# Three of four squared MLP blocks turned by VectorE and SBUF transfers instead of TensorE

## The chip, the core and the metric

The kernel runs on 1 core of one Trainium2 chip. The metric is device time in microseconds (us): median 2288.86 of 3 runs (2288.14 to 2289.62). Engines are named as the profile does: PE is TensorE (PEld its weight loads), DVE VectorE, ACT ScalarE, POOL GpSimd, SP SyncE; SPq, POOLq and ACTq are the queues from which an engine issues DMAs.

## The reference, cut to what matters

Two transformer blocks on one sequence of 256 tokens, width 2048, float32. The change lies in the MLP of the first:

```python
u = _rmsnorm(h, norm_mlp_g)                     # (256, 2048)
a = jnp.einsum('bsd,df->bsf', u, w_up)          # (256, 8192)
a = jnp.square(jax.nn.relu(a))
h = h + jnp.einsum('bsf,fd->bsd', a, w_down)    # back to (256, 2048)
```

Before it come the first block's projection, Fourier mixing and attention; behind it the second block: gated linear attention, a convolution and a SwiGLU, with six modulation vectors made from `c @ w_mod` (2048 x 12288).

## The kernel before, in words

**Products.** Every large product is made of groups: a group is 512 rows of a weight matrix by 512 columns, 1 MB, which SP loads in two pieces of 512 KB (`load`, L380) into a ring of 4 groups (`wring`). ACT rounds a piece to `whi` (L575 or L565), DVE makes the remainder `wlo` (L1090), and PE does, for each piece, 4 matmuls of 128x512 with hi times `whi` (L1798), 4 with lo times `whi` (L1802) and 4 with hi times `wlo` (L1807). `whi` and `wlo` hold two groups. So SP may load a group when DVE is done with the one four before (`lo_done`, L382), and ACT may round a piece when PE has finished the same piece two groups before (`piece_multiplied`, L574).

**The MLP.** It runs in `MLP_CHUNKS` = 4 chunks of 32 groups (`mlp_chunk`, on ACT L839, DVE L1383, PE L2056). In this text "group 0" to "group 31" are those of a chunk in the order in which PE multiplies them. Groups 0 to 15 are four blocks of `w_up` (`j` = 0 to 3, four groups each, operand `ahi`/`alo`). After each of them ACT writes relu of the sums to `blk2` (L823) and the square of that to `blk` (L827), 256 tokens by 512 columns. Groups 16 to 31 are four blocks of `w_down`; their operand `xhi`/`xlo` is the squared block with tokens in the free dimension, so the block must be turned. PE turns it: `turn_rows(blk, 2)` (L2081, eight 128x128 transposes at L1869) behind group 4j+1, for j = 1 to 4, that is behind groups 5, 9, 13 and 17. ACT rounds the two PSUM banks to `xhi` (L591), DVE takes the remainder `xlo` (L1152). Group 16 multiplies block 0, group 17 block 1, group 18 block 2, group 19 block 3, and so on for each column block.

**How far ahead ACT and DVE are.** The opening of the kernel (L697 to L709) has ACT and DVE do two groups more than PE, and they stay two ahead in their program order. Where the code of `mlp_chunk` says `g` on ACT and DVE, the group handled is group g+2. The turned block of j = 4 is therefore rounded (`g % 4 == 1`) behind ACT's rounding of group 19, whose second piece waits for PE to finish group 17.

**The modulation vectors.** Beside the MLP, POOL loads `w_mod` in steps of 512 KB into a ring of two (L460), and DVE adds each step to `macc` with `scalar_tensor_tensor` (L1116, L1120; 2 or 4 instructions a step). `MLP_MODS` gives the step behind each group on DVE, `MLP_REDUCED = {7: SC2, 15: SC1, 22: GT1, 30: SH2}` the groups behind which PE turns the finished `macc` (`reduce_mod`, L1873, L1880; it waits for `mod_acc`). SC1 has the double steps (4 instructions): they stand on DVE behind groups 9 to 16, and PE reduces them behind group 15.

**The second block's SwiGLU** already turns three of four blocks another way: DVE turns 32x32 squares (L1693), POOL moves the strips with sixteen transfers of 32 KB within SBUF (L551), ACT rounds the placed rows (L1018) and DVE takes the remainder (L1698).

Of the kernel before, what the change touches and what calls it, by code (L numbers as in the profile page):

```python
# [55 lines left out]
X_HI = 2 * (2 * KG - 1) + 4 * KG + 8 * MLP_CHUNKS + 2 * KG + 2 * KG + 8  # L56
# [54 lines left out]
def two_blocks(nc, x, ctx_in, w_in, w_fourier, w_out, w_up, w_down, w_mod, w_in2, w_out2, w_gate,  # L111
               w_up2, w_down2, vectors, gates_w, mid_g, final_g, tables, fourier_tables, attn_tables, out):
    ctx = ExitStack()
    with ctx:
# [91 lines left out]
        with ExitStack() as ph:  # L206
# [47 lines left out]
            sem(n) for n in ("squares_turned", "rows_moved", "moved_hi", "moved_lo"))  # L254
        out_s = sem("out_s")
# [112 lines left out]
        T_O = 8 + 8 + 8 * MLP_CHUNKS + 8 + 8 + 4 + BANKS["out"] + sum(  # L368
# [3 lines left out]
        MOVES = 16 * 16  # L372
        block = ctx.enter_context(nc.Block())
# [3 lines left out]
        def _(sp):  # L377
# [28 lines left out]
            with c.loop(sp, MLP_CHUNKS, g=32) as i:  # L406
                for j in range(4):
                    block_of(w_up, i * D + j * NB)
                for n in range(4):
                    block_of(w_down, n * NB, kg0=i * 4)  # L410
# [144 lines left out]
        def _(act):  # L555
# [262 lines left out]
            def relu_square(j, first=False):  # L818

                if first:  # L820
                    act.wait_ge(rstd_done, 2)
                for t in range(T):
                    last = act.activation(blk2[:, t, :], acc[:, 2 * (j % 2) + t, :], ACT.Relu, scale=rstd[:, 1, t:t + 1])  # L823
                last.then_inc(blk_half, 1)
                c.add("half")
                act.wait_ge(blk_half, c.at("half"))
                act.activation(blk[:, :, :], blk2[:, :, :], ACT.Square).then_inc(blk_ready, 1)  # L827
                c.add("blk")

# [9 lines left out]
            def mlp_chunk(first=False, last=False):  # L839

                def round_group(g):
                    round_piece(0)
                    if g - 1 in MLP_REDUCED and not (last and MLP_REDUCED[g - 1] == SH2):
                        sum_mod(MLP_REDUCED[g - 1] == SC1)
                    round_piece(1)
                    if last and g in CTX_TURNS:
                        round_modulated(ahi, CTX_TURNS[g], CTX_TURNS[g] + 1)

                for j in range(8):
                    round_group(4 * j)  # L850
                    if j >= 5:
                        square_block(j - 5, first)
                    round_group(4 * j + 1)
                    if first and j == 0:
                        root(1)
                    if 1 <= j <= 4:
                        round_banks(xhi, 4 * (j - 1), 2)
                    round_group(4 * j + 2)
                    round_group(4 * j + 3)
                    if j < 4:  # L860
                        wait_block(2)
                        relu_square(j, first and j == 0)
                square_block(3, first)
# [3 lines left out]
            with c.loop(act, MLP_CHUNKS - 1, 1, g=32, q=8, half=4, blk=4, ha=4, ssq=4 * T, mt=5):  # L867
                mlp_chunk()
# [211 lines left out]
        def _(dve):  # L1080
# [301 lines left out]

            def mlp_chunk(i, first=False, last=False):  # L1383
                done = 0
                for g in range(32):
# [7 lines left out]
                    if g % 4 == 1 and 1 <= j <= 4:  # L1393
                        remain_banks(xhi, xlo, 4 * (j - 1), 2)
# [25 lines left out]
            with c.loop(dve, MLP_CHUNKS - 1, 1, g=32, q=8, hi=8, m=32, ma=80, mt=5, msum=5 * KG) as i:  # L1420
# [346 lines left out]
        def _(pe):  # L1767
# [288 lines left out]
            def mlp_chunk(first=False, last=False):  # L2056
# [6 lines left out]
                for j in range(8):  # L2063
# [10 lines left out]
                    for kg in range(3):  # L2074
                        multiply(hi, lo, (kg,), 4, pair)
# [3 lines left out]
                        if kg == 1 and 1 <= j <= 4:  # L2079
# [13 lines left out]
                c.add("blk", 4)  # L2093

            mlp_chunk(True)
            with c.loop(pe, MLP_CHUNKS - 1, 1, g=32, q=8, ma=80, ha=4, half=4, blk=4):
# [331 lines left out]
```

## Time and profile before

| | |
|---|---|
| median of 3 runs | 2288.86 us |
| span of the profiled execution | 2285.8 us |
| what a run has around that span (difference of the two) | 3.1 us |
| PE busy | 2266.4 us (99%) |
| DVE busy, ACT busy | 1556.3 (68%), 1109.7 (49%) |
| granted PE clock, mean of the span | 0.997 |
| PE idle in the MLP | 1.0 us |

The page and the answers show one execution of the program. Its own device time stands nowhere apart from the span; the 3.1 us lie around the span. The MLP lasts from about 295 to about 1015 us. A row of a timeline gives the start, how long the merged instructions lasted from the first start to the last end, and how many they are; PE's matmuls overlap, so the distance between the starts of two rows is what a row costs. `[x <-E line]` behind a row is the engine's idle time before it and who ended it.

### The profile page before, as it was taken

The page shows a single profiled execution, that of the slowest core. Times are in us where ns is not written, and L with a number is a line of the kernel's source. Part 1 is how long each engine was busy: PE and PEld are TensorE (multiplying, and loading weights), DVE is VectorE, ACT ScalarE, POOL GpSimd, SP SyncE. Part 2 cuts the span into 40 slices and gives each one's busy share as a digit, 9 for nine tenths or more (in the row PEclk, how much of TensorE's full clock was granted, in tenths as well). Part 3 has the DMA queues.
Part 4 walks back from the last instruction along what each step waited for, and adds up shares of the span by engine and source line. Part 5 has one row for each costly group of instructions (what it writes and reads, how often), then busy time and mean ns, then how long its engine had stood idle before and what let it go on. Part 6 is the DMA issues. An engine that isn't in the chain of part 4 may idle for free.

```text
span 2285.8 us, 28964 instructions
## 1 busy us (share of the span) xinstructions
PE 2266.4 (99%) x10345; PEld 1864.5 (82%) x10345; DVE 1556.3 (68%) x1869; ACT 1109.7 (49%) x1531; POOL 223.5 (10%) x361
## 2 busy tenths in 40 slices
PE   9999999999999999999999999999999999999998
PEld 7888888888888888888878877787888888888886
DVE  7886778778867877887767664556555545555556
ACT  6446455555545545545463463545444344444444
POOL 0121001111111111110011000000210011100110
PEclk9999999999999999999999999999999999999999
DMA  8983679978888888886677664564665666656663
GB/s 311 331 272 97 206 235 320 317 267 293 275 281 287 273 301 269 272 280 215 220 242 245 209 203 129 186 220 158 210 203 194 207 207 198 207 185 201 195 195 126
DMA packets 250005, 528.12 MB, mean 231 GB/s; under 512 B 22144, under 2 KB 22544, under 8 KB 248592
## 3 DMA queue, kind: packets, MB, share of 16 engines
q1 hardware_dynamic: 214256, 405.32, 54.2%
q0 software_dynamic: 33664, 116.17, 14.8%
q10 hardware_dynamic: 1952, 4.85, 0.6%
q8 instruction: 84, 1.38, 0.2%
q14 instruction: 49, 0.40, 0.1%
HBM read 517.87 MB, written 4.21 MB: 228 GB/s over the span
## 4 chain that ended last, share of the span: by engine, by line
PE 97%; DVE 1%; ACT 1%; DMA 0%; issue 0%; SPq 0%; ACTq 0%; DVEq 0%; POOLq 0%
PE acc L1798 30%; PE acc L1807 29%; PE acc L1802 29%; PE tp L1869 2%; PE m L1880 1%; PE acc L1820 0%; PE acc L1825 0%; PE acc L1830 0%; PE tp L2206 0%; PE tp L2224 0%; PE tp L2218 0%; PE acc L2000 0%; PE tp L2131 0%; PE acc L1853 0%; PE acc L1851 0%
## 5 line engine op out<-in xcount | busy, mean ns | idle before, releaser
L1090 DVE TENSOR_TENSOR wlo<-wring,whi 128x1024 fp32r<-128x1024 f32 x762 | 919.5, 1216 | 562.6 <-ACT whi L565 455.4
L565 ACT ACTIVATE whi<-wring 128x1024 fp32r<-128x1024 f32 (+1 forms) x510 | 532.1, 1047 | 720.4 <-PE acc L1807 719.3
L1798 PE MATMUL acc<-whi,xhi 128*128 128x512 f32 x2056 | 558.5, 393 | 0.1
L1802 PE MATMUL acc<-whi,xlo 128*128 128x512 f32 x2056 | 550.0, 389 | 0.0
L1807 PE MATMUL acc<-wlo,xhi 128*128 128x512 f32 x2056 | 549.9, 389 | 0.0
L1802 PEld LDWEIGHTS acc<-whi,xlo 128*128 128x128 f32 x2056 | 386.0, 188 | 81.1
L1807 PEld LDWEIGHTS acc<-wlo,xhi 128*128 128x128 f32 x2056 | 386.0, 188 | 80.7
L1798 PEld LDWEIGHTS acc<-whi,xhi 128*128 128x128 f32 x2056 | 381.2, 188 | 86.3 <-issue 9.0
L575 ACT ACTIVATE whi<-wring 128x1024 fp32r<-128x1024 f32 x266 | 280.8, 1059 | 319.8 <-PE acc L1807 318.1
L1120 DVE SCALAR_TENSOR_TENSOR macc<-mring,csil,macc 128x512 f32<-128x512 f32 x480 | 344.0, 747 | 29.3 <-DMA mring<-w_mod 23.0
L460 POOL DMA_DIRECT2D mring<-w_mod x192 | 138.9, 724 | 1047.4 <-DVE macc L1120 998.9
L1798 PE MATMUL acc<-whi,ahi 128*128 128x512 f32 x608 | 164.9, 393 | 0.0
L1807 PE MATMUL acc<-wlo,ahi 128*128 128x512 f32 x608 | 162.8, 389 | 0.0
L1802 PE MATMUL acc<-whi,alo 128*128 128x512 f32 x608 | 162.7, 389 | 0.0
L1802 PEld LDWEIGHTS acc<-whi,alo 128*128 128x128 f32 x608 | 114.1, 188 | 24.1
L1807 PEld LDWEIGHTS acc<-wlo,ahi 128*128 128x128 f32 x608 | 114.1, 188 | 24.0
L1798 PEld LDWEIGHTS acc<-whi,ahi 128*128 128x128 f32 x608 | 112.3, 188 | 22.1 <-issue 0.2
L551 POOL DMA_DIRECT2D tmpT<-blk x128 | 62.6, 498 | 517.9 <-DVE blk L1693 516.6
L1798 PE MATMUL acc<-whi,bhi 128*128 128x512 f32 x336 | 90.1, 390 | 0.0
L1807 PE MATMUL acc<-wlo,bhi 128*128 128x512 f32 x336 | 89.8, 389 | 0.0
L1802 PE MATMUL acc<-whi,blo 128*128 128x512 f32 x336 | 89.8, 389 | 0.0
L1802 PEld LDWEIGHTS acc<-whi,blo 128*128 128x128 f32 x336 | 63.1, 188 | 13.1
(277 smaller groups left out, 1313.7 us busy)
## 6 DMA issues: line engine op xcount, KB each, us to landing
wring<-w_up SPq DMA_DIRECT2D x216, 512.0 KB, 4.7
wring<-w_down SPq DMA_DIRECT2D x216, 512.0 KB, 5.1
mring<-w_mod POOLq DMA_DIRECT2D x192, 512.0 KB, 5.3
wring<-w_in SPq DMA_DIRECT2D x184, 512.0 KB, 5.2
wring<-w_gate SPq DMA_DIRECT2D x88, 512.0 KB, 4.3
wring<-w_out SPq DMA_DIRECT2D x64, 512.0 KB, 4.9
tmpT<-blk POOLq DMA_DIRECT2D x128, 32.0 KB, 3.4
gbig<-ctx_in POOLq DMA_DIRECT2D x2, 1024.0 KB, 8.1
```

The lines of the kernel that those rows point to most:

```text
L460: pool.dma_start(mring[:, c.slot("m", MSLOTS), :, :], w_mod_v[s, :, :, bass.ds(i * NB + kind * D, NB)])\
L551: pool.dma_start(placed[32 * j:32 * j + 32, i, :], strips[32 * i:32 * i + 32, j, :]).then_inc(rows_moved, 16)
L565: act.activation(whi[:, piece_slot(c, piece), 0:half], wring[:, g4, piece * half:(piece + 1) * half], ACT.Copy).then_inc(hi_done, 1)
L575: act.activation(whi[:, piece_slot(c, piece), :], wring[:, g4, piece * half:(piece + 1) * half], ACT.Copy).then_inc(hi_done, 1)
L1090: dve.tensor_tensor(wlo[:, h4, 0:half], wring[:, g4, piece * half:(piece + 1) * half], whi[:, h4, 0:half].bitcast(F32), ALU.subtract).then ...
L1120: dve.scalar_tensor_tensor(macc[:, who, :], mring[:, m2, kt, :], csil[:, who, k:k + 1], macc[:, who, :], ALU.mult, ALU.add).then_inc(mod_a ...
L1798: pe.matmul(acc[:, 2 * pair + t, :], hi[:, tile, t * P:(t + 1) * P], whi[:, h4, w], start=(tile == starts), stop=False)
L1802: pe.matmul(acc[:, 2 * pair + t, :], lo[:, tile, t * P:(t + 1) * P], whi[:, h4, w], start=False, stop=False)
L1807: last = pe.matmul(acc[:, 2 * pair + t, :], hi[:, tile, t * P:(t + 1) * P], wlo[:, h4, w], start=False, stop=(tile == stops))
L1869: last = pe.transpose(tp[:, q, j * S + t * P:j * S + (t + 1) * P], src[:, t, f:f + P], ident)
L1880: last = pe.transpose(bank[:, j * P:(j + 1) * P], macc[:, who, j * P:(j + 1) * P], ident)
```

## The change: blocks 0 to 2 are turned on DVE and moved by SP

Block 3 of each chunk stays on PE (behind group 17). Blocks 0, 1 and 2 go another way. ACT writes relu and square both in `blk`. DVE turns the block in 32x32 squares into `blk2` (`turn_relu`, two instructions), behind its remainders of groups 7, 11 and 15. SP, behind its loads of groups 9, 13 and 17, waits for that and issues sixteen transfers of 32 partitions by 1 KB from `blk2` to `tmpT` (`move_strips`). ACT rounds the placed rows in four instructions (`round_relu`) behind groups 11, 15 and 19, and DVE takes four remainders (`remain_relu`) behind the same groups. PE waits for `relu_lo` before group 16 (blocks 0 and 1) and before group 18 (block 2).

```diff
@@ sync
+            def move_strips():
+                sp.wait_ge(relu_turned, c.at("rs", T, T))
                 for j in range(4):
-                    block_of(w_up, i * D + j * NB)
+                    for i in range(4):
+                        sp.dma_start(placed[32 * j:32 * j + 32, i, :], strips[32 * i:32 * i + 32, j, :]).then_inc(relu_moved, 16)
+                c.add("rs")
+            def up_block(i, j):
+                v = w_up.rearrange("(g k p) n -> g p k n", k=KG, p=P)
+                for kg in range(KT // KG):
+                    load(v[kg, :, :, bass.ds(i * D + j * NB, NB)])
+                    if j >= 2 and kg == 1:
+                        move_strips()
...
                 for n in range(4):
-                    block_of(w_down, n * NB, kg0=i * 4)
+                    v = w_down.rearrange("(g k p) n -> g p k n", k=KG, p=P)
+                    for kg in range(KG):
+                        load(v[bass.ds(i * 4 + kg, 1), :, :, n * NB:(n + 1) * NB].rearrange("a p k n -> (a p) k n"))
+                        if n == 0 and kg == 1:
+                            move_strips()
@@ scalar
+                if j:
+                    act.wait_ge(relu_turned, c.at("rt", T, T))
+                    c.add("rt")
                 for t in range(T):
-                    last = act.activation(blk2[:, t, :], acc[:, 2 * (j % 2) + t, :], ACT.Relu, scale=rstd[:, 1, t:t + 1])
+                    last = act.activation(blk[:, t, :], acc[:, 2 * (j % 2) + t, :], ACT.Relu, scale=rstd[:, 1, t:t + 1])
...
+            def round_relu(tile):
+                act.wait_ge(relu_moved, c.at("rm", RELU_MOVES, RELU_MOVES))
+                for k in range(KG):
+                    act.activation(xhi[:, tile + k, :].rearrange("p (t i b) -> p t i b", t=T, i=4),
+                                   moved[:, k], ACT.Copy).then_inc(relu_hi, 1)
+                c.add("rm")
...
-                    if 1 <= j <= 4:
-                        round_banks(xhi, 4 * (j - 1), 2)
+                    if 2 <= j <= 4:
+                        round_relu(4 * (j - 2))
+                    if j == 4:
+                        round_banks(xhi, 12, 2)
@@ vector
+            def turn_relu():
+                dve.wait_ge(blk_ready, c.at("blk", 1))
+                dve.wait_ge(relu_moved, c.at("rt", 0, RELU_MOVES))
+                for t in range(T):
+                    dve.transpose(turned[:, t], blk[:, t, :].rearrange("p (k j b) -> p k j b", k=KG, j=4)).then_inc(relu_turned, 1)
+                c.add("rt")
+            def remain_relu(tile):
+                for k in range(KG):
+                    dve.wait_ge(relu_hi, c.at("rk", 1))
+                    dve.tensor_tensor(xlo[:, tile + k, :].rearrange("p (t i b) -> p t i b", t=T, i=4), moved[:, k],
+                                      xhi[:, tile + k, :].bitcast(F32).rearrange("p (t i b) -> p t i b", t=T, i=4),
+                                      ALU.subtract).then_inc(relu_lo, 1)
+                    c.add("rk")
...
                     if g % 4 == 1 and 1 <= j <= 4:
-                        remain_banks(xhi, xlo, 4 * (j - 1), 2)
+                        if j >= 2:
+                            remain_relu(4 * (j - 2))
+                        if j < 4:
+                            turn_relu()
+                        c.add("blk")
+                        if j == 4:
+                            remain_banks(xhi, xlo, 12, 2)
@@ tensor
+                        if j == 4 and kg in (0, 2):
+                            pe.wait_ge(relu_lo, c.at("rs", KG * (2 if kg == 0 else 3), KG))
                         multiply(hi, lo, (kg,), 4, pair)
...
-                        if kg == 1 and 1 <= j <= 4:
+                        if kg == 1 and j == 4:
                             pe.wait_ge(blk_ready, c.at("blk", j))
                             turn_rows(blk, 2)
```

The counts of the bank semaphores follow (`X_HI`, `T_O`, `q`, `hi`). Where instructions stand now is shown at two places. First DVE from its remainders of group 15 to the last SC1 step, behind those of group 16, first chunk, before (the `macc` rows are the last two of the eight steps that PE's reduction behind group 15 waits for):

```order
L1090 TENSOR_TENSOR wlo<-wring,whi 128x1024 [waits hi_done] x2
L1152 TENSOR_TENSOR xlo<-tp,xhi 128x512 [waits tp_hi] x2
L1120 SCALAR_TENSOR_TENSOR macc<-mring,csil,macc 128x512 [waits mod_acc,step_landed0]
L1120 SCALAR_TENSOR_TENSOR macc<-mring,csil,macc 128x512 [waits mod_acc] x3
L1090 TENSOR_TENSOR wlo<-wring,whi 128x1024 [waits hi_done] x2
L1120 SCALAR_TENSOR_TENSOR macc<-mring,csil,macc 128x512 [waits mod_acc,step_landed1]
L1120 SCALAR_TENSOR_TENSOR macc<-mring,csil,macc 128x512 [waits mod_acc] x3
```

And the same stretch now:

```order
L1126 TENSOR_TENSOR wlo<-wring,whi 128x1024 [waits hi_done] x2
L1430 TENSOR_TENSOR xlo<-tmpT,xhi 128x256 [waits relu_hi] x4
L1424 STREAM_TRANSPOSE blk<-blk 128x4x4x32 [waits relu_moved,blk_ready]
L1424 STREAM_TRANSPOSE blk<-blk 128x4x4x32
L1156 SCALAR_TENSOR_TENSOR macc<-mring,csil,macc 128x512 [waits mod_acc,step_landed0]
L1156 SCALAR_TENSOR_TENSOR macc<-mring,csil,macc 128x512 [waits mod_acc] x3
L1126 TENSOR_TENSOR wlo<-wring,whi 128x1024 [waits hi_done] x2
L1156 SCALAR_TENSOR_TENSOR macc<-mring,csil,macc 128x512 [waits mod_acc,step_landed1]
L1156 SCALAR_TENSOR_TENSOR macc<-mring,csil,macc 128x512 [waits mod_acc] x3
```

The one pair of bank remainders (L1152 before, now L1188) has become four remainders of the moved block 1 and two turns of block 2, ahead of the last two SC1 steps.

Second PE behind group 17, first chunk, before:

```order
L1869 MATMUL tp<-tabs,blk 128x128 [waits tp_free,blk_ready]
L1869 MATMUL tp<-tabs,blk 128x128 x3
L1869 MATMUL tp<-tabs,blk 128x128 [waits tp_free]
L1869 MATMUL tp<-tabs,blk 128x128 x3
L1798 MATMUL acc<-whi,xhi 128x512 [waits hi_done]
L1798 MATMUL acc<-whi,xhi 128x512 x3
L1802 MATMUL acc<-whi,xlo 128x512 x4
L1807 MATMUL acc<-wlo,xhi 128x512 [waits lo_done]
```

And the same place now:

```order
L1928 MATMUL tp<-tabs,blk 128x128 [waits tp_free,blk_ready]
L1928 MATMUL tp<-tabs,blk 128x128 x3
L1928 MATMUL tp<-tabs,blk 128x128 [waits tp_free]
L1928 MATMUL tp<-tabs,blk 128x128 x3
L1857 MATMUL acc<-whi,xhi 128x512 [waits hi_done,relu_lo]
L1857 MATMUL acc<-whi,xhi 128x512 x3
L1861 MATMUL acc<-whi,xlo 128x512 x4
L1866 MATMUL acc<-wlo,xhi 128x512 [waits lo_done]
```

The first matmul of group 18 has gained a wait, for `relu_lo`. What gives it stands on DVE here, behind the remainders of group 19:

```order
L1126 TENSOR_TENSOR wlo<-wring,whi 128x1024 [waits hi_done] x2
L1430 TENSOR_TENSOR xlo<-tmpT,xhi 128x256 [waits relu_hi] x4
L1188 TENSOR_TENSOR xlo<-tp,xhi 128x512 [waits tp_hi] x2
L1156 SCALAR_TENSOR_TENSOR macc<-mring,csil,macc 128x512 [waits mod_acc,step_landed0]
L1156 SCALAR_TENSOR_TENSOR macc<-mring,csil,macc 128x512 [waits mod_acc]
```

The four remainders of block 2 (L1430) follow the two remainders of group 19 (L1126), and those of block 3 (L1188) follow them.

## Rows read from the trace of the kernel before

**Rows 1.** The page: span, busy times, granted clock, the chain that ended last.

```profile
span 2285.8 us, 28964 instructions
...
PEclk9999999999999999999999999999999999999999
...
PE 97%; DVE 1%; ACT 1%; DMA 0%; issue 0%; SPq 0%; ACTq 0%; DVEq 0%; POOLq 0%
```

**Rows 2.** Waits in 290 to 1010 us: who waited, us in total, times, longest.

```profile
PE m L1880 <- DVE macc L1120: 1.0, 1, 1.0
```

**Rows 3.** Timeline of PE round group 17 of the second chunk: start us, us.

```profile
600.90 1.07 PE L1807 MATMUL acc<-wlo,xhi 128*128 128x512 f32 x4
601.81 1.03 PE L1869 MATMUL tp<-tabs,blk 128*128 128x128 f32 x8
602.60 1.17 PE L1798 MATMUL acc<-whi,xhi 128*128 128x512 f32 x4
603.61 1.07 PE L1802 MATMUL acc<-whi,xlo 128*128 128x512 f32 x4
```

**Rows 4.** Timeline of ACT and DVE in the same place.

```profile
602.01 1.06 ACT L575 ACTIVATE whi<-wring 128x1024 fp32r<-128x1024 f32 x1 [1.66 <-PE acc L1807]
603.10 1.23 DVE L1090 TENSOR_TENSOR wlo<-wring,whi 128x1024 fp32r<-128x1024 f32 x1 [0.99 <-ACT whi L575]
604.24 1.28 DVE L1152 TENSOR_TENSOR xlo<-tp,xhi 128x512 fp32r<-128x512 f32 x2
```

**Rows 5.** Timeline of DVE in the SwiGLU, where blocks are moved.

```profile
1634.78 1.42 DVE L1698 TENSOR_TENSOR blo<-tmpT,bhi 128x256 fp32r<-128x256 f32 x4
1646.90 1.30 DVE L1693 STREAM_TRANSPOSE blk<-blk 128x512 f32<-128x512 f32 x2
1648.13 1.18 DVE L1090 TENSOR_TENSOR wlo<-wring,whi 128x1024 fp32r<-128x1024 f32 x1
```

**Rows 6.** Timeline of DVE, groups 11 to 16 of the second chunk, and PE's reduction.

```profile
556.83 1.23 DVE L1090 TENSOR_TENSOR wlo<-wring,whi 128x1024 fp32r<-128x1024 f32 x1 [0.36 <-ACT whi L575]
559.17 2.73 DVE L1120 SCALAR_TENSOR_TENSOR macc<-mring,csil,macc 128x512 f32<-128x512 f32 x4
575.19 2.73 DVE L1120 SCALAR_TENSOR_TENSOR macc<-mring,csil,macc 128x512 f32<-128x512 f32 x4
577.84 1.22 DVE L1090 TENSOR_TENSOR wlo<-wring,whi 128x1024 fp32r<-128x1024 f32 x1
587.00 2.73 DVE L1120 SCALAR_TENSOR_TENSOR macc<-mring,csil,macc 128x512 f32<-128x512 f32 x4
590.01 1.04 PE L1880 MATMUL m<-tabs,macc 128*128 128x128 f32 x8
```

**Rows 7.** DMA issues: SP's (ns min/median/max), POOL's sixteen (timeline), landing of SP's loads.

```profile
L387 SPq DMA_DIRECT2D wring<-w_up x216: 367/373/1625, 292.7 to 2181.1; - x108
1692.02 7.81 POOL L551 DMA_DIRECT2D tmpT<-blk  x16 [35.71 <-DVE blk L1693]
wring<-w_down SPq DMA_DIRECT2D x8, 512.0 KB, 6.1
```

**Rows 8.** Timeline of PE: a pause in the attention, and the SwiGLU's opening.

```profile
196.47 0.63 PE L2025 MATMUL tp<-tabs,blk 128*128 128x128 f32 x4 [1.33 <-ACT blk L782]
1547.50 0.66 PE L2305 MATMUL m<-tabs,u_ffn 128*128 128x128 f32 x4 [1.07 <-DVE h L1618]
1549.64 0.98 PE L2305 MATMUL tp<-tabs,u_ffn 128*128 128x128 f32 x4 [1.49 <-DVE u_ffn L1645]
1552.05 2.07 PE L1820 MATMUL acc<-whi,xhi 128*128 128x512 f32 x4 [0.57 <-ACT xhi L600]
1557.03 1.07 PE L1820 MATMUL acc<-whi,xhi 128*128 128x512 f32 x4
```

**Rows 9.** Stretches of that opening: us, PE PEld DVE ACT POOL busy, PEclk, DMA share, GB/s.

```profile
1550.00:1552.00 2.00, 1.47 (x7) 1.07 (x6) 1.67 (x4) 0.88 (x2) 0.00 (x0) 0.50 0.00 0
1556.00:1558.00 2.00, 2.00 (x9) 1.61 (x8) 1.64 (x2) 0.33 (x1) 0.00 (x0) 0.84 0.86 277
```

More of the change, by code:

```diff
@@ L55 @@
 WARM = 4
-X_HI = 2 * (2 * KG - 1) + 4 * KG + 8 * MLP_CHUNKS + 2 * KG + 2 * KG + 8
+MLP_MOVED = 3
+X_HI = 2 * (2 * KG - 1) + 4 * KG + 2 * MLP_CHUNKS + 2 * KG + 2 * KG + 8
 H0 = 2
@@ L254, in two_blocks @@
             sem(n) for n in ("squares_turned", "rows_moved", "moved_hi", "moved_lo"))
+        relu_turned, relu_moved, relu_hi, relu_lo = (
+            sem(n) for n in ("relu_turned", "relu_moved", "relu_hi", "relu_lo"))
         out_s = sem("out_s")
@@ L366, in two_blocks @@
         BANKS = {"z": 1, "suffix": 1, "ctx_state": 1, "state": 2, "turn": 1, "out": 1, "conv": 2}
-        T_O = 8 + 8 + 8 * MLP_CHUNKS + 8 + 8 + 4 + BANKS["out"] + sum(
+        T_O = 8 + 8 + 2 * MLP_CHUNKS + 8 + 8 + 4 + BANKS["out"] + sum(
             BANKS.get(step[0], 0) for steps in BESIDE[1].values() for step in steps)
@@ L372, in two_blocks @@
         MOVES = 16 * 16
+        RELU_MOVES = 16 * 16
         block = ctx.enter_context(nc.Block())
@@ L405, in _ @@
                     block_of(w_out, i * (2 * NB) + j * NB)
-            with c.loop(sp, MLP_CHUNKS, g=32) as i:
+            def move_strips():
+                sp.wait_ge(relu_turned, c.at("rs", T, T))
                 for j in range(4):
-                    block_of(w_up, i * D + j * NB)
-                for n in range(4):
-                    block_of(w_down, n * NB, kg0=i * 4)
+                    for i in range(4):
[7 more added lines that the diff above has]
+                        move_strips()
+            with c.loop(sp, MLP_CHUNKS, g=32, rs=MLP_MOVED) as i:
+                for j in range(4):
+                    up_block(i, j)
+                for n in range(4):
+                    v = w_down.rearrange("(g k p) n -> g p k n", k=KG, p=P)
[3 more added lines that the diff above has]
+                            move_strips()
             for names in (C_IN, X_IN):
@@ L826, in relu_square @@
                 act.wait_ge(blk_half, c.at("half"))
-                act.activation(blk[:, :, :], blk2[:, :, :], ACT.Square).then_inc(blk_ready, 1)
+                act.activation(blk[:, :, :], blk[:, :, :], ACT.Square).then_inc(blk_ready, 1)
                 c.add("blk")
+            def round_relu(tile):
[4 more added lines that the diff above has]
+                c.add("rm")
             def square_block(n, first):
@@ L866, in _ @@
             root_and_scale(2, u_g, u_g)
-            with c.loop(act, MLP_CHUNKS - 1, 1, g=32, q=8, half=4, blk=4, ha=4, ssq=4 * T, mt=5):
+            with c.loop(act, MLP_CHUNKS - 1, 1, g=32, q=2, half=4, blk=4, ha=4, ssq=4 * T, mt=5, rt=MLP_MOVED, rm=MLP_MOVED):
                 mlp_chunk()
@@ L1419, in _ @@
             norm_scale(2, u_g, u_g)
-            with c.loop(dve, MLP_CHUNKS - 1, 1, g=32, q=8, hi=8, m=32, ma=80, mt=5, msum=5 * KG) as i:
+            with c.loop(dve, MLP_CHUNKS - 1, 1, g=32, q=2, hi=2, m=32, ma=80, mt=5, msum=5 * KG, blk=4, rt=MLP_MOVED,
+                        rk=KG * MLP_MOVED) as i:
                 mlp_chunk(i)
@@ L2093, in mlp_chunk @@
                 c.add("blk", 4)
+                c.add("rs", MLP_MOVED)
             mlp_chunk(True)
-            with c.loop(pe, MLP_CHUNKS - 1, 1, g=32, q=8, ma=80, ha=4, half=4, blk=4):
+            with c.loop(pe, MLP_CHUNKS - 1, 1, g=32, q=2, ma=80, ha=4, half=4, blk=4, rs=MLP_MOVED):
                 mlp_chunk()
```

## The prediction

> **What bounds the kernel now.** I read the page first: the chain that ended last is 97% PE and the granted clock is full in every slice [rows 1]. So PE's own instructions set the time, and one that is taken from PE is worth its full length as long as PE finds its operands. I then read the waits inside the MLP: PE waits once in 720 us, 1.0 us, for DVE's `macc` [rows 2]. The reader is to see two things: PE has no slack to give, and the only engine it ever waits for there is DVE with the modulation steps. So I asked of each edit what it takes from PE, and then at each wait of PE how near DVE and ACT already are, by laying the timelines of PE, ACT and DVE side by side in the second chunk.
>
> **What is removed.** Behind group 17 the turn is eight transposes. PE starts them at 601.81, the next matmuls at 602.60 and the ones after those at 603.61; a plain row of four takes 0.91 (600.90 to 601.81) [rows 3]. From 601.81 to 603.61 are 1.80; less 0.91, a turn costs 0.89. Three of four turns go in each of four chunks: 12 x 0.89 = 10.7 us off PE.
>
> **What DVE gets.** In place of two bank remainders it has, behind group 7 the two square turns, behind 11 and 15 four remainders and two turns, behind 19 four remainders more than before. The SwiGLU has the same instructions: four remainders 1.42, two turns 1.23 (1646.90 to 1648.13) [rows 5]; the bank remainders took 1.28 by their row [rows 4], less the 0.08 by which instructions overlap on DVE (a row of 2.73 is followed 2.65 later [rows 6]), 1.20. Behind groups 11 and 15 that is 1.42 + 1.23 - 1.20 = 1.45 more each, behind 7 nothing.
>
> **First place: PE's reduction behind group 15.** PE starts it at 590.01, and the last SC1 step on DVE runs from 587.00 to 589.73 [rows 6]: a margin of 0.28 now. With the change PE arrives earlier by three turns, 2.69, at 587.32. DVE arrives so: its second remainder of group 11 starts 0.90 earlier than 556.83 (one turn, behind group 5, is gone from PE, which ACT and DVE follow), at 555.93. From there DVE finds all inputs ready and is never idle. A remainder costs 1.14 (603.10 to 604.24) [rows 4], a double step 2.65 (575.19 to 577.84) [rows 6]. Group 11: 1.14 + 1.42 + 1.23 + 2.65 = 6.44. Groups 12, 13, 14: each 2 x 1.14 + 2.65 = 4.93, 14.79. Group 15: 2 x 1.14 + 1.42 + 1.23 + 2.65 = 7.58. Group 16: 2 x 1.14 + 2.73 = 5.01. Sum 33.82, end at 589.75. So the step ends where it ended before, and PE waits 589.80 - 587.32 = 2.5 us. The earlier turns bought nothing but a wait: 4 x 2.5 = 10.0 us. The idle time that DVE had between these groups (0.36 in the row of 556.83) is the only cover, and the sum has used it.
>
> **Second place: group 18.** PE's first matmul of group 18 waits for the remainders of block 2. ACT handles that block behind its rounding of group 19, whose second piece waits for PE's end of group 17 (ACT starts at 602.01, released by L1807) [rows 4]. DVE takes the remainder of that piece at 603.10 and would start on the block at 604.24; with four remainders of 1.42 it ends at 605.66, and PE goes on at about 605.71. PE, with the turn of block 3 done, would have gone on at 602.60 [rows 3]. That is 3.1 us of idling, which no amount of lead on SP or DVE can shorten, because it begins with PE's own end of group 17. The pattern is the same in all four chunks: 4 x 3.1 = 12.4 us. Block 3 follows on DVE at 605.7 and is wanted behind group 18: hidden.
>
> **SP's queue.** Each block costs SP a wait and sixteen issues. The wait itself holds the next load: load 14 may be issued when group 10's remainders are done, but stands behind the sixteen transfers, which wait for DVE's turn of block 1 at 559.7 (555.93 + 1.14 + 1.42 + 1.23 = 559.72). An issue takes 0.37 by SP's own rows, and 0.49 as POOL does sixteen in 7.81 [rows 7]: 5.9 to 7.8 us. SP comes free at 565.7 to 567.6, and the two pieces of load 14 land, at up to 6.1 [rows 7], by 571.5 to 574.2. DVE wants their rounded form at 572.25 and 573.39. So this costs DVE's dense run between 0 and 1.5 us, and PE's wait behind group 15 grows by as much. PE itself wants group 14 later than that. I take 0.7, near the middle, since the two issue rows lie equally near: 4 x 0.7 = 2.8. Loads 10 and 18 have the same delay but no dense run behind them; ACT's rounding of group 19 is reached in time. The transfers move 512 KB a block beside 1 MB a group; the transfers of the SwiGLU keep no PE waiting in the trace.
>
> **Back.** The one wait of 1.0 for `macc` [rows 2] comes late in the last chunk and goes, since PE arrives later there: -1.0.
>
> **The sum without the clock.** -10.7 + 10.0 + 12.4 + 2.8 - 1.0 = +13.5.
>
> **The clock.** PE idled 1.07 and 1.49 within 4 us at the SwiGLU's opening, with only transposes between, and the granted clock then stood at 0.50, the 1.2 GHz level, from 1550 until into the stretch from 1556 (0.84) [rows 8, 9]. At that level three rows of four 128x512 matmuls took 1552.05 to 1557.03, 4.98, where 3 x 0.91 = 2.73 is usual: 2.3 us lost. A pause of 1.33 in the attention brought no fall [rows 8 and 1]. The new pauses, 2.5 and 3.1, lie between: as long as the two of the opening together, but single. A fall can cost nothing, or 2.3 as here, or up to half of the 7 us at 0.5, 3.4. Of the eight pauses I let two be followed by a fall, because the longer kind is nearer to what the opening shows and its place differs from chunk to chunk: 2 x 2.3 = 4.6.
>
> By the Trainium skill, page "TensorE: Matmul & The Clock Gate", part "PE-mode transpose", transposes do not count as work for the clock gate as matmuls do. The turn of block 3 stands directly before the pause at group 18 and the reduction's transposes directly behind the one at group 15, so by that rule every pause is longer than its idle time and all eight could be followed by a fall; the opening, where only transposes broke the pause, agrees. That is the second rival.
>
> **Forecast.** +13.5 + 4.6 = +18.1 on the span of 2285.8, 2303.9, and with the 3.1 around it (the difference of span and median) 2307.
>
> **Rivals.**
> 1. Only the two waits, no fall and no late load: 13.5 - 2.8 = +10.7, 2299.6. For it: single pauses never brought a fall in this trace. Against it: none of them was as long.
> 2. All pauses are followed by a fall: 13.5 + 8 x 2.3 = +31.9, 2321. For it: the opening [rows 8, 9]. Against: the pause of 1.33.
> 3. DVE keeps up and only group 18 waits: -10.7 + 12.4 - 1.0 = +0.7, 2289.6, no change. It decides by whether DVE ends SC1 by 587.3; it would have to do 33.8 us of work in 31.4.
> 4. The other side: the remainders of block 2 are ready before PE ends group 17, because ACT's order is not two groups ahead as I read it, or PE's count is met by an earlier block. Then PE only waits behind group 15, -10.7 + 10.0 - 1.0 = -1.7, 2287.2, and with rival 3 in force as well -10.7, 2278. It decides at one point, whether ACT's rounding before the block is that of group 19. Rows 4 speak against it: ACT's rounding in front of the banks starts with PE's end of group 17.
> 5. SP's transfers are slower than POOL's, say twice, 15.6 us a block: loads 10, 14 and 18 come 8 later and PE itself waits about 4 at each: 12 x 4 = 48 more, some 2355. No row shows such an issue but the longest, 1.6 [rows 7].
>
> **Chances.** Forecast (two waits, one to four falls, loads a little late) 0.55; rival 1, 0.16; rival 2, 0.13; rival 3, 0.07; rival 4, 0.05; rival 5, 0.04. A measurement can tell about 0.2%, 4.6 us, from no change: below 2284.3 is faster, above 2293.4 slower. Faster has rival 4's larger half, 0.03; the same has the rest of it and rival 3's, 0.08; slower the rest, 0.89. For the range I take rival 1's end with a fall of the waits by a few us, 2296, and rival 2's end, 2322; outside are rivals 3, 4 and 5.
>
> **What would show it.** In the profile after: PE idle before L1939 (`m<-tabs,macc`) by DVE's `macc`, four times, 2.5 to 4 each; PE idle before L1857 in front of group 18 by DVE's `xlo` L1430, four times, 3.1; PE's transposes of `blk` in the MLP down from 128 to 32; SP's rows L415, 192 of them, near 0.4 each; the clock below 9 in slices of the MLP if falls come. No idle time before group 18 would refute the second place, and idle time there above 5 would mean late transfers or loads. If PE's idle time before L1939 is under 1, DVE had more room than its rows show. Idle time of PE released by `whi` or by a load would speak for rival 5.

## The result, and the profile after

The changed kernel takes 2355.68 us (median of 4 runs, 2354.0 to 2357.8) against 2289.24 for the kernel before on the same chip (4 runs): ratio 1.0289, 95% interval 1.0275 to 1.0303. It is slower by 66 us, where 18 were forecast, and outside the forecast range. The page after, against [rows 1] (the last row is the chain that ended last):

```profile
span 2353.7 us, 29072 instructions
...
PE 2282.5 (97%) x10249; PEld 1871.6 (80%) x10249; DVE 1571.5 (67%) x1917; ACT 1110.9 (47%) x1555; POOL 223.3 (9%) x361
...
PEclk9999999999899999989999999999999999999999
...
PE 81%; SPq 5%; DVE 5%; DMA 4%; issue 3%; ACT 2%; DVEq 0%; ACTq 0%; POOLq 0%
```

PE's share of the chain fell from 97% to 81%, and SP's queue, at 0% before, has 5%. The waits in 290 to 1080 us, against [rows 2] (who waited, us in total, times, longest):

```profile
ACT whi L598 <- DMA wring<-w_up: 74.6, 24, 11.6
ACT whi L598 <- DMA wring<-w_down: 42.1, 5, 11.6
PE m L1939 <- DVE macc L1156: 23.7, 5, 6.9
...
PE acc L1857 <- DVE xlo L1430: 15.4, 4, 4.2
PE acc L1857 <- ACT whi L598: 11.6, 5, 3.3
...
PE acc L1866 <- DVE wlo L1126: 1.6, 1, 1.6
```

PE waits 52.3 us in place of 1.0. The two waits forecast are there (23.7 and 15.4), and beside them 13.2 us for `whi` and `wlo`. The first two rows are the news: ACT now waits 116.7 us for loads of weights, which it never did in this stretch before.

PE in the second chunk, against [rows 3] and the last row of [rows 6]:

```profile
600.78 2.07 PE L1857 MATMUL acc<-whi,ahi 128*128 128x512 f32 x4 [2.87 <-ACT whi L598]
...
618.41 1.97 PE L1939 MATMUL m<-tabs,macc 128*128 128x128 f32 x8 [3.64 <-DVE macc L1156]
620.03 2.05 PE L1857 MATMUL acc<-whi,xhi 128*128 128x512 f32 x4
621.88 1.91 PE L1861 MATMUL acc<-whi,xlo 128*128 128x512 f32 x4
...
632.86 1.03 PE L1928 MATMUL tp<-tabs,blk 128*128 128x128 f32 x8
637.48 2.01 PE L1857 MATMUL acc<-whi,xhi 128*128 128x512 f32 x4 [3.58 <-DVE xlo L1430]
```

Three pauses in 40 us, and behind each a row of four matmuls takes 1.9 to 2.1 where [rows 3] have 1.07. The granted clock there (the stretch, its us, PE PEld DVE ACT POOL busy, PEclk, DMA share, GB/s, as in [rows 9]) is 0.50, the 1.2 GHz level:

```profile
618.00:622.00 4.00, 3.59 (x13) 3.21 (x14) 3.77 (x5) 0.11 (x1) 0.72 (x1) 0.50 0.50 133
```

SP's queue in that chunk, and its issue times (ns min/median/max) against [rows 7]:

```profile
557.68 10.52 SPq L415 DMA_DIRECT2D tmpT<-blk  x16
568.46 5.04 SPq L391 DMA_DIRECT2D wring<-w_up  x8
584.23 10.42 SPq L415 DMA_DIRECT2D tmpT<-blk  x16
594.90 2.15 SPq L391 DMA_DIRECT2D wring<-w_up  x4
597.31 2.71 SPq L391 DMA_DIRECT2D wring<-w_down  x4
610.84 10.01 SPq L415 DMA_DIRECT2D tmpT<-blk  x16
...
L415 SPq DMA_DIRECT2D tmpT<-blk x192: 507/590/987, 360.7 to 1010.2; - x192
```

Sixteen transfers take SP 10.0 to 10.5 us, 0.65 each, not 5.9 to 7.8. Behind each of the first two sixteens, SP issues eight pieces of weights within 5 us: they were overdue. What that does on ACT and DVE:

```profile
572.25 1.06 ACT L598 ACTIVATE whi<-wring 128x1024 fp32r<-128x1024 f32 x1 [4.09 <-DMA wring<-w_up]
...
599.67 1.06 ACT L598 ACTIVATE whi<-wring 128x1024 fp32r<-128x1024 f32 x1 [9.28 <-DMA wring<-w_up]
...
581.57 1.43 DVE L1430 TENSOR_TENSOR xlo<-tmpT,xhi 128x256 fp32r<-128x256 f32 x4
582.91 1.29 DVE L1424 STREAM_TRANSPOSE blk<-blk 128x512 f32<-128x512 f32 x2
```

The first row is group 10, the second group 14. The four remainders and the two turns take what the SwiGLU's rows gave [rows 5].

**The loop.** The chain that ended last, read in this stretch (start us, us, what; steps between are left out), shows why this repeats:

```profile
584.23 0.52 SPq L415
...
594.90 0.38 SPq L391
595.46 5.45 DMA wring<-w_up
601.02 1.07 ACT whi L598
...
609.60 1.23 DVE blk L1424 x2
610.84 0.51 SPq L415
```

From the first transfer of block 1 (584.23) to that of block 2 (610.84) are 26.6 us: sixteen transfers until SP issues load 14 (594.90, 10.7); its pieces land and ACT rounds the second from 601.02 (6.1); DVE's remainders, modulation steps and its turn of block 2, in program order, until SP is released (9.8). PE needs 21.8 for the four groups of that round (eight pieces of 2.72). So each round is 4.8 longer than PE's work, and PE's lead over the loads is used up after one. The round before it, from block 0 (557.68) to block 1, is 26.6 long as well.

### The profile page after: what moved, and what is told of

It is laid out like the page before. It is cut to its first block, busy times and chain, and to the rows that moved or that the text cites. A ratio compares the mean times of both kernels' runs of the same rounds, so it can differ in the third digit from the quotient of the medians.

```text
span 2353.7 us, 29072 instructions
## 1 busy us (share of the span) xinstructions
PE 2282.5 (97%) x10249; PEld 1871.6 (80%) x10249; DVE 1571.5 (67%) x1917; ACT 1110.9 (47%) x1555; POOL 223.3 (9%) x361
## 3 DMA queue, kind: packets, MB, share of 16 engines
q1 hardware_dynamic: 223472, 411.63, 52.3%
## 4 chain that ended last, share of the span: by engine, by line
PE 81%; SPq 5%; DVE 5%; DMA 4%; issue 3%; ACT 2%; DVEq 0%; ACTq 0%; POOLq 0%
PE acc L1857 24%; PE acc L1861 24%; PE acc L1866 24%; SPq L415 5%; DMA wring<-w_up 2%; DVE macc L1156 2%; DMA mring<-w_mod 1%; DVE wlo L1126 1%; PE tp L1928 1%; ACT whi L598 1%; DMA wring<-w_down 1%; ACT m L636 1%; DVE xlo L1430 1%; DVE blk L1424 1%; PE acc L1879 0%
## 5 line engine op out<-in xcount | busy, mean ns | idle before, releaser
L1126 DVE TENSOR_TENSOR wlo<-wring,whi 128x1024 fp32r<-128x1024 f32 x762 | 917.7, 1216 | 616.9 <-ACT whi L588 454.7
L1857 PE MATMUL acc<-whi,xhi 128*128 128x512 f32 x2056 | 565.8, 397 | 15.5 <-DVE xlo L1430 15.4
L1857 PEld LDWEIGHTS acc<-whi,xhi 128*128 128x128 f32 x2056 | 385.6, 190 | 103.9 <-DVE xlo L1430 16.4
L1857 PE MATMUL acc<-whi,ahi 128*128 128x512 f32 x608 | 166.4, 396 | 11.6 <-ACT whi L598 11.6
```

The costliest lines, as they stand in the source:

```text
L1126: dve.tensor_tensor(wlo[:, h4, 0:half], wring[:, g4, piece * half:(piece + 1) * half], whi[:, h4, 0:half].bitcast(F32), ALU.subtract).then ...
L1857: pe.matmul(acc[:, 2 * pair + t, :], hi[:, tile, t * P:(t + 1) * P], whi[:, h4, w], start=(tile == starts), stop=False)
```

## The experiments

For each kernel in it the table has the median, the span of its profiled execution less 2285.8, and an account of that difference: the turns removed (-10.7), PE's waits in 290 to 1080 us less the 1.0 of before, and the slower clock, (1 - mean granted clock) x span, less the 6.9 of before (clock 0.997). A clock has three digits, so each product is good to 1.2 and the difference of two to 2.3. The span is that of one execution: in `e5`, `e7` and `e11` it was the slowest of its kernel, so there it stands 4 to 6 us further from the kernel before than the median does.

| kernel | median | span, more | waits | clock (mean) | sum |
|---|---|---|---|---|---|
| after | 2355.7 | +67.9 | +51.3 | +30.8 (0.984) | +71.4 |
| e1_no_transfers | 2309.9 | +22.0 | +20.9 | +9.3 (0.993) | +19.5 |
| e2_transfers_later | 2311.6 | +25.1 | +22.7 | +11.6 (0.992) | +23.6 |
| e3_block2_sooner | 2337.9 | +47.1 | +40.2 | +16.4 (0.990) | +45.9 |
| e4_both | 2295.1 | +6.1 | +11.2 | +4.6 (0.995) | +5.1 |
| e5_reduction_later | 2299.2 | +17.8 | +16.7 | +11.5 (0.992) | +17.5 |
| e6_half_transfers | 2318.1 | +29.9 | +27.0 | +11.6 (0.992) | +27.9 |
| e7_one_transfer | 2314.3 | +30.6 | +25.4 | +13.9 (0.991) | +28.6 |
| e9_reductions_later | 2279.6 | -7.9 | +0.7 | +2.2 (0.996) | -7.8 |
| e11_no_transfers_reductions_later | 2278.0 | -4.8 | +1.8 | +2.3 (0.996) | -6.6 |

The account closes within 4 us for each, so nothing large is outside these three terms.

**No transfers.** SP neither waits nor issues, and ACT and DVE no longer wait for the strips to land (`relu_moved`); all their instructions stay, on rows that nothing has placed.

```diff
-                sp.wait_ge(relu_turned, c.at("rs", T, T))
-                for j in range(4):
-                    for i in range(4):
-                        sp.dma_start(placed[...], strips[...]).then_inc(relu_moved, 16)
...
-                act.wait_ge(relu_moved, c.at("rm", RELU_MOVES, RELU_MOVES))
...
-                dve.wait_ge(relu_moved, c.at("rt", 0, RELU_MOVES))
```

> The changed kernel without its 192 transfers of strips on SP and without the waits for them (SP neither waits nor issues; ACT and DVE still do all their instructions, on rows that nothing has placed). Theory (SP's queue: each block holds the next loads by SP's wait for the turn plus sixteen issues of 0.65 us, 10.4 in all, the weights come late, and DVE's steps before the reduction come late with them): the idle times before groups 10 to 14 go, the wait before the reduction behind group 15 falls from 3.6 to 6.9 to the 2.5 that DVE's own added work makes, the one before group 18 stays at 3.6 to 4.2; 2300 to 2312. Rival (DVE's added work, not SP, makes the wait before the reduction): it stays at 4 to 7 and the time stays above 2335.

2309.94 (ratio 1.0094, 1.0077 to 1.0110), in the range that was expected. Of the 66 us, some 45 go with the transfers. The landing of the strips, which this edit also took out of ACT's and DVE's way, is not what costs: in the changed kernel no wait of ACT or DVE in 290 to 1080 us ends with a `tmpT` transfer. What is left is what steps 1 to 3 of the prediction were about (steps are its parts: 1 what is removed, 2 the first place, 3 the second place, 4 SP's queue, 5 "Back"), and PE's rows in its second chunk show it. The wait before group 18 is shorter than the 3.6 to 4.2 expected here, 2.9 to 3.2:

```profile
597.42 1.09 PE L1933 MATMUL m<-tabs,macc 128*128 128x128 f32 x8 [2.10 <-DVE macc L1151]
...
613.18 1.90 PE L1851 MATMUL acc<-whi,xhi 128*128 128x512 f32 x4 [2.88 <-DVE xlo L1424]
```

**Transfers later.** The same sixteen transfers, behind loads 11, 15 and 19 in place of 9, 13 and 17 (`kg == 3` for `kg == 1` in both places).

> The sixteen transfers of a block stand two loads later on SP (behind the loads of groups 11, 15, 19 and not 9, 13, 17), so that SP no longer stands in a wait with two free places in the ring. Theory (the wait for the turn costs more than the issues): SP still loses 10.4 us to each block, but the loads behind it have some 8 us of room left, so PE never waits for whi or wring; the reduction waits about 2.5, group 18 waits for block 2: near the time of the run without transfers, within 8 us, 2300 to 2315, with a longer wait at group 18 if the transfers of block 2 end after PE's group 17. Rival (the issue time by itself makes loads late): 2335 to 2360.

2311.61 (1.0096, 1.0080 to 1.0113), in the range of the theory and 1.7 above the kernel without any, a difference inside the intervals. This kernel moves the same bytes over the same DMA engines as the changed one, so the traffic of the strips is not what costs 45 us either; their place in SP's queue is. SP in the second chunk:

```profile
547.52 11.22 SPq L415 DMA_DIRECT2D tmpT<-blk  x16
559.00 10.13 SPq L391 DMA_DIRECT2D wring<-w_up  x8
570.62 10.83 SPq L415 DMA_DIRECT2D tmpT<-blk  x16
581.72 9.64 SPq L391 DMA_DIRECT2D wring<-w_down  x8
```

Sixteen transfers take about as long as before (10.8 to 11.2), and eight loads behind them now take some 10 us to issue: they are no longer a burst but go out as their slots come free. Why two groups of place matter: block 1 is turned behind the remainders of group 11. Load 14, which stood behind its transfers, has its slot when group 10 is done, so it waited for a later event than its own and for 10.4 us of issue more. Load 16 has its slot when group 12 is done, and DVE ends that at 575.5, 5 us behind the turn (570.6): half of the issues fill time in which SP would have waited. The load then goes out 6 us behind its slot (581.7), and in this kernel ACT waits for no load of weights.

**One transfer, eight transfers.** At the changed kernel's place, `range(1)` and `range(1)`, or `range(4)` and `range(2)`, for the two loops over transfers, and `RELU_MOVES` to suit.

> The changed kernel with a single transfer per block, so that SyncE still waits for VectorE's turn at the same place, but issues for 0.65 us instead of 10.4 (the rest of each block stays unplaced). Theory (the 10.4 us of issue are what the loads have no slack for): 2306 to 2315, near the kernel without transfers (2309.9). Rival (the wait for the turn): over 2335.

> The changed kernel with 8 of a block's 16 transfers (half of each block stays unplaced), at the place that the change has. Theory (the loads are late by the wait for the turn and then the 10.4 us in which SyncE issues 16 transfers; without these 5.2 us most of it goes): load 14 lands about 5 us sooner, TensorE's waits for whi go and with them most of the slower clock, 2310 to 2328. Rival (waiting for the turn alone makes the loads late, the number of transfers doesn't matter): 2345 to 2356.

One transfer 2314.33 (1.0102, 1.0087 to 1.0118), eight 2318.13 (1.0128, 1.0112 to 1.0143), both where the theory had them. The kernel before was 1.4 slower in these two comparisons than in that of the kernel without transfers, so each is best taken over its own: 21.17 us without transfers, 24.15 with one, 27.95 with eight, 66.44 with sixteen. The wait for the turn with one issue costs 3.0, inside the intervals, the next seven 3.8 together, and the last eight 38.5. That is the loop: at eight, SP's part is 5.2 us in place of 10.7,

```profile
567.43 4.96 SPq L415 DMA_DIRECT2D tmpT<-blk  x8
572.64 2.11 SPq L391 DMA_DIRECT2D wring<-w_up  x4
```

so the chain of the round would be 26.6 - 5.5 = 21.1, an estimate just under PE's 21.8. The rounds as traced are 23.1 to 23.5, with eight transfers and with one: their length no longer hangs on the number of transfers. ACT's wait for weights is 12.4 us in place of 116.7.

**Block 2 sooner.** ACT rounds block 2 behind group 18, not 19, and DVE takes its remainders behind those of group 18.

```diff
-                    if 2 <= j <= 4:
+                    if 2 <= j <= 3:
                         round_relu(4 * (j - 2))
...
                     round_group(4 * j)
+                    if j == 4:
+                        round_relu(8)
...
+                    if g == 16:
+                        remain_relu(8)
```

> The changed kernel with ACT's rounding and DVE's remainders of block 2 one group sooner (behind group 18 in place of 19), nothing else. Theory: the 15.4 us of idle time before group 18 go, and the falls of the clock behind it with them (up to 2 to 3 us each): 2355 less 15 to 27, 2328 to 2342. Rival (PE would wait for late loads there anyway): 2350 to 2357.

2337.94 (1.0219, 1.0202 to 1.0236), as expected. PE's wait for the remainders of block 2 (`xlo`) goes from 15.4 to 2.0, the one for `macc` stays (26.5, from 23.7).

**Both of these.**

> Transfers two loads later and block 2 rounded one group sooner. What is left is the wait before the reduction behind group 15, about 2.5 a chunk, against 10.7 saved: if the clock does not fall 2287 to 2291, with a fall behind each of the four waits up to 2298. If block 2's transfers, now behind the load of group 19, end too late for the sooner place, PE waits some 2 to 4 before group 18 again: 2295 to 2310.

2295.07 (1.0028, 1.0017 to 1.0038), the end of the expectation with falls of the clock. One kind of wait is left, 12.2 us for `macc` in five places.

**Reduction later.** As both, with the reduction of SC1 behind group 16.

```diff
-                    **{g: (GT1, 2 if g == 18 else 1) for g in range(15, 22)},
+                    **{g: (GT1, 2 if g in (18, 20) else 1) for g in range(16, 22)},
-        MLP_REDUCED = {7: SC2, 15: SC1, 22: GT1, 30: SH2}
+        MLP_REDUCED = {7: SC2, 16: SC1, 22: GT1, 30: SH2}
```

> Transfers behind loads 11, 15 and 19, the third block rounded sooner, and the 32-step modulation group now runs behind groups 7 to 14 as before but is reduced behind group 16 (the next kind's steps follow from 16 on, two of them doubled). E4, the same without the last edit, took 2295.1 with 12.2 us of TensorE's wait for macc and about 4.6 us of slower clock more than before. Theory (VectorE is full only in the stretch up to group 16, one group more lets it catch up): both go, 2276 to 2284, faster than before. Rival (the wait is only pushed one group on, or to group 18): 2291 to 2298.

2299.16 (1.0042, 1.0029 to 1.0056): the theory missed, the rival came. PE's wait went, and came back behind group 22:

```profile
638.96 0.65 PE L1943 MATMUL m<-tabs,macc 128*128 128x128 f32 x4 [4.21 <-DVE macc L1158]
...
624.33 1.54 DVE L1158 SCALAR_TENSOR_TENSOR macc<-mring,csil,macc 128x512 f32<-128x512 f32 x2 [2.49 <-DMA mring<-w_mod]
```

With two doubled groups so near each other, DVE waits for the steps' own loads; `mring` has room for two.

**Reductions later.** The same with one doubled group for each kind:

```diff
+                    **{g: (GT1, 2 if g == 20 else 1) for g in range(16, 23)},
+                    **{g: (SH2, 2 if g == 27 else 1) for g in range(23, 30)}}
+        MLP_REDUCED = {7: SC2, 16: SC1, 23: GT1, 30: SH2}
```

> As E5 (transfers behind loads 11, 15 and 19, third block sooner, 32-step reduction behind group 16), but the next kind's steps run behind groups 16 to 22 with one of them doubled (at 20) and are reduced behind 23, and the last kind's behind 23 to 29 with one doubled (at 27). E5 took 2299.2: its wait for macc (16.3 us) had gone from the first reduction to the one behind group 22, ahead of which two steps in a row were doubled and VectorE waited for their loads. Theory (no group has then more steps than the loads follow): both waits go, with the slower clock behind them, 2276 to 2284, faster than before. Rival (the wait turns up at another group once more): 2290 to 2298.

2279.63 (5 runs, 2279.24 to 2281.20; ratio 0.9959, 0.9945 to 0.9972), 0.4% faster than the kernel before, as the theory had it. PE's waits in the stretch are 1.7 us in three places, and behind group 17 nothing is left between the turn of block 3 and group 18:

```profile
599.87 1.03 PE L1932 MATMUL tp<-tabs,blk 128*128 128x128 f32 x8
600.66 1.17 PE L1861 MATMUL acc<-whi,xhi 128*128 128x512 f32 x4
```

**What the transfers and the table are worth there.** The same without transfers, and the kernel before with only this table.

> E9 without its transfers (the third part of e1 and the moved reductions together; the turned squares are not put into place). Theory (at their new place the transfers cost next to nothing): within 3 us of E9, 2274 to 2283. Rival (48 transfers of 32 KB per chunk still delay the modulation loads or the weights): more than 5 us below E9.

> The kernel before (TensorE turns all four blocks), with only E9's table of modulation steps (reductions behind groups 16, 23 and 30). It tells whose the gain of E9 is (2279.6 against 2289.6). Theory (TensorE waits 1.0 us for macc in the kernel before, so the table has nothing to gain there, and E9's gain is that of the turns removed): 2287 to 2291. Rival (the table alone brings it): 2282 or less.

Without transfers 2278.04 (0.9948, 0.9933 to 0.9964): 1.6 less than with them, inside the intervals. The table alone 2290.83 (1.0005, 0.9996 to 1.0014): nothing. Both are as their theories had them. So the 10 us are those of the turns taken from PE. By the Trainium skill, page "VectorE: DVE Perf Modes", section "Rules for kernel authors", a 128x128 transpose goes to TensorE where PSUM will do as its target; here, where TensorE is the bound and DVE and SP have time, the other way is worth 10 us.

**Filled pauses.** TensorE multiplies the identity ahead of its waits, so that it does not pause.

```diff
+            def fill(n):
+                pe.wait_ge(tp_free, c.at("q", 1))
+                for _ in range(n):
+                    pe.matmul(tp[:, c.slot("q", 2), 0:P], ident, ident, start=True, stop=True)
```

> The changed kernel, with matmuls of the identity put in on TensorE ahead of the two waits: 28 (about 3.6 us) before the one for macc behind group 15, 26 (about 3.3 us) before the one for xlo at group 18, into the bank that the next turn uses. They add nothing to the result and stay within the waits as traced (3.6 to 6.9 and 3.6 to 4.2 us). Theory (the granted clock falls after TensorE has paused, and about 30 of the 67 us are matmuls at the lower clock): the falls behind these two waits go, 15 to 25 us come back, 2328 to 2342. Rival (the falls have another cause, or the waits for late loads bring them all the same): 2350 to 2362.

2382.13 (1.0403), outside both the theory and the rival, a miss of the experiment: each such matmul is two records, the fill of 28 took 6.4 us, and the one before group 18 waited itself for the bank of block 3's turn (20.4 us in four places). It shows only that the clock holds behind a filled pause. Again with 18, before the reduction alone:

> The changed kernel with fill ahead of the wait for macc behind group 15 only, 18 matmuls of the identity with itself, which ran as two records of 0.114 us each in E8, so about 4.1 us beside waits of 3.6 to 6.9 us. Nothing of it is in the result. E8 put in twice the length meant (6.4 us in one place, 5.9 behind another wait in the other). Theory (the clock falls after a pause; each of the four falls behind this wait costs 2.9 us, worked out from the rows at 618.41 us): 8 to 12 us come back, 2343 to 2348. Rival (the fall comes whether TensorE pauses there or not): 2354 to 2360.

2355.63 (1.0287, 1.0271 to 1.0302): nothing came back, though the clock did. The time is in the rival's range, but not for the rival's reason, that the fall comes all the same. The mean granted clock is 0.989 instead of 0.984, which by the account is 12 us. PE in its second chunk:

```profile
608.96 4.18 PE L2117 MATMUL tp<-tabs 128*128 128x128 f32 x36
615.51 1.09 PE L1940 MATMUL m<-tabs,macc 128*128 128x128 f32 x8 [2.37 <-DVE macc L1157]
...
634.85 2.07 PE L1858 MATMUL acc<-whi,xhi 128*128 128x512 f32 x4 [6.44 <-DVE xlo L1431]
```

The reduction's eight take 1.09, not 1.97; and the next wait, before group 18, is 6.4 instead of 3.6. Over the four chunks that wait grew from 15.4 to 24.6 us. The account closes here too: -10.7, waits +43.0, clock +19.0 and four fills of 4.1, together +67.7 against +67.4. So the chain through SP, ACT and DVE sets the pace between these two places, and PE at full clock only reaches the next wait sooner. That means that what the account puts down to the falls behind the reduction is not a saving to be had in the changed kernel. By the Trainium skill, page "TensorE: Matmul & The Clock Gate", section "HAM oscillation — how this bites in real kernels", PE restarts at the lower clock behind each wait for data and pays for it each time; the page says so of a kernel that waits for a DMA at each of its steps. The trace agrees in the three rows at 600.78, 618.41 and 637.48 us, but not behind every pause (2.08 us before 795.22 us is followed by a granted clock of 1.00); that PE pays each time, this run does not bear out where the next operand is late as well.

## Why the prediction was wrong

**Step 1, turns removed: right.** -10.7 was forecast. The best version has +0.7 of waits and +2.2 of clock in the account and is 7.9 shorter, which leaves 10.8 for the turns; the same without transfers leaves 8.9. Either is good to 2.3.

**Step 2, the wait before the reduction: mechanism and size right, by itself.** Forecast 2.5 in each chunk. Without transfers it is 2.09 to 2.15 in each. In the changed kernel it is 3.6 to 6.9, 22.0 in four, since ACT and DVE come to this stretch late. In the first chunk it is longer also where no load is late (3.83 with the transfers later, 4.71 with both edits); why was not tried.

**Step 3, the wait before group 18: right.** Forecast 3.1. Without transfers 2.88 to 3.21, 11.9 in four; in the changed kernel 15.4.

**Step 4, SP's queue: this failed.** The prediction gave it 2.8 us in all; the difference between the changed kernel and the one without transfers is 45.7 (45.3 with each taken over its own kernel before), of which the waits are 30.4. Without this term and with its clock term the prediction makes +15.3, where the kernel without transfers has +21.2; the rest of the miss is here. The step had two errors that matter. The price of an issue was taken from rows of other kinds, 0.37 (a load of 512 KB) and 0.49 (POOL); SP's small transfers take 0.65, so SP's part is 10.4 us. It also left out, in "DVE wants their rounded form", ACT's own rounding of a piece, 1.06 by [rows 4]. And it followed load 14 once, to DVE's dense run and no further ("loads 10 and 18 have the same delay but no dense run behind them"). But load 14 feeds the remainders and steps behind which DVE turns block 2, and that turn releases the next sixteen transfers and load 18. With the rest of the round as traced (26.6 - 10.7 = 15.9), even the forecast's issues of 5.9 to 7.8 would make 21.8 to 23.7 against PE's 21.8, an estimate: no slack, at the price assumed. Eight transfers against sixteen show how steep it is from there. Rival 5 named this end, "some 2355", with 0.04. Its time was met by chance: it wanted issues of 15.6 us a block and 4 us of PE's idling at each load; they took 10.4, and `whi` and `wlo` cost PE only 13.2.

**Step 5, the 1.0 back: wrong and small.** The late wait of the last chunk is there, 1.50 without transfers, 1.68 with.

**The clock.** Forecast 4.6, two falls in eight pauses. Without transfers the account has 9.3 (good to 2.3). There the four pauses of 2.9 to 3.2 before group 18 were each followed by rows of 1.80 to 2.07, and of the four of 2.1 before the reduction one was (411.04: the eight transposes at 1.09, the next row at 1.94): five falls of eight where the sum had two, so the term was too small by half even without late loads. The size of a fall, 2.3, was about right (9.3 / 5 = 1.9).

The length of a pause does not decide alone. In the four kernels without transfers, with them later, with one and with eight, all sixteen pauses of 2.87 to 3.21 before group 18 were followed by a fall, but only seven of the sixteen of 2.09 to 3.93 before the reduction. With eight transfers the reduction's pause of 3.84 is followed by rows of 1.17 and 1.08 (granted clock 1.00 from 411 to 414 us), the pause of 3.21 before group 18 by half clock (0.50 from 427 to 430).

Both kinds of pause stand beside eight transposes, before group 18 ahead of the pause and at the reduction behind it. So rival 2's rule, that transposes do not keep the clock up, is not settled: all pauses before group 18 go with it, more than half of those before the reduction do not.

The prediction's list of what would show it served: idle time of PE released by `whi`, named there as a sign for rival 5, is in the profile, and SP's rows L415 are 0.59 where it said near 0.4.

**The 3.1 around the span.** It set a median beside the span of another run. Each run's own two differ by 1.7 in the changed kernel (2355.41 and 2353.7) and by 2.1 in the kernel before, so this term was 1 us too large.

**Left open.** Why a transfer of 32 KB costs SP more to issue than one of 512 KB was not tried with other shapes. Which of the two errors of step 4 counts for more was not tried either: no run has sixteen transfers at 0.37 to 0.49. The parts of 30.8 that the clock costs in the changed kernel at places other than the reduction were not separated.

## What to carry to other kernels

A queue that both waits for an engine and feeds it closes a loop: add up one whole round (wait, issues, landing, the work up to the next release) and compare it with what the bound engine needs for the same round; below it the added work costs almost nothing, above it every round pays the excess. Put such transfers behind the load whose own slot comes free after the event they wait for, not before it. And a wait removed by moving one step may turn up at the next step that was squeezed to make room.

## What the runs showed of the hardware

- SP issues a transfer of 32 partitions by 1 KB within SBUF in 0.59 us (median of 192), one every 0.65; a load of 512 KB takes it 0.37. So a sixteenth of the bytes did not make an issue shorter; the size of the transfers was not varied by itself.
- 192 such transfers, where SP has time for them, cost the kernel 1.6 us (2279.63 against 2278.04), less than the runs can tell from nothing.
- A 128x128 matmul of the float32 identity is two records, one every 0.114 us at the 2.4 GHz level (56 in 6.4).
- The pause before the reduction, filled with these matmuls, is followed by rows at full clock in all four chunks (1.09 for eight transposes), unfilled, in the changed kernel, in none (1.97).
- Pauses of PE of nearly the same length end at either clock: of sixteen of 2.09 to 3.93 us before the reduction seven were followed by a fall, of sixteen of 2.87 to 3.21 before group 18 all (four kernels).
